# Spectral filter, small layers and first weight unit placed earlier among the conditioning units of a macaron DiT layer's first stage

## The reference

```python
mx = [m[:, None, :] for m in jnp.split(jax.nn.silu(c) @ ada_w[l] + ada_b[l], N_MOD, axis=-1)]
mc = jnp.split(jax.nn.silu(c_ctx) @ ada_w[l] + ada_b[l], N_MOD, axis=-1)
...
x = x + 0.5 * mx[2] * _swiglu(_modulate(_rmsnorm(x, norm_ffn1[l]), mx[0], mx[1]),
                              ffn1_w1[l], ffn1_w3[l], ffn1_w2[l])
...
# _hyena_spectrum
hid = jnp.sin(freq * (z @ w1 + b1))
hid = jnp.sin(freq * (hid @ w2 + b2))
hid = jnp.sin(freq * (hid @ w3 + b3))
h = (hid @ w_out).reshape(n, 2, 2, HY_WIDTH)
...
l1 = jnp.sum(jnp.abs(h_fwd), axis=0) + jnp.sum(jnp.abs(h_bwd), axis=0)
filt = jnp.concatenate([h_fwd, jnp.zeros((1, 2, HY_WIDTH), F32), h_bwd[::-1]], axis=0) / l1
return jnp.fft.rfft(filt, axis=0)
```

## Time and profile before

| what | value |
|---|---|
| runs of the kernel before | 3018.55, 3019.62, 3019.79 us (median 3019.62) |
| the profiled execution, as timed | 3019.63 us |
| span of its profile | 3017.8 us |
| TensorE matmuls busy | 2969.1 us, 98% of the span |
| VectorE, ScalarE, GpSimd busy | 68%, 38%, 5% |
| DMA over the span | 559.07 MB, mean 185 GB/s |
| granted TensorE clock, mean | 0.997 |

### The profile page before, as it was taken

One profiled execution on the slowest core, in us unless ns is written; L12 is line 12 of the kernel. 1 busy time (PEld: TensorE's weight loads), 2 busy tenths in 40 slices (PEclk: granted clock), 3 DMA queues, 4 the chain that ended last, 5 costly groups with the idle time before them and its releaser, 6 DMA issues. The chain is left out here.

```text
span 3017.8 us, 42600 instructions
## 1 busy us (share of the span) xinstructions
PE 2969.1 (98%) x15878; PEld 2528.7 (84%) x15878; DVE 2049.1 (68%) x2663; ACT 1160.7 (38%) x1477; POOL 147.7 (5%) x181
## 2 busy tenths in 40 slices
PE   7999999999999999999999999999999999999998
PEld 3588888888888888888889999999998888888886
DVE  4598667676766677673477767778866666666667
ACT  4332222222222222222248777754345444444444
POOL 1000000000000000000000033430000000000001
PEclk9999999999999999999999999999999999999999
DMA  9965546354466758563345554555565666666664
GB/s 370 327 209 188 181 134 202 128 178 146 157 221 221 255 168 282 186 228 102 95 98 167 171 166 148 153 152 180 158 203 168 188 192 190 188 193 189 189 193 147
DMA packets 369856, 559.07 MB, mean 185 GB/s; under 512 B 18175, under 2 KB 260216, under 8 KB 368840
## 3 DMA queue, kind: packets, MB, share of 16 engines
q1 hardware_dynamic: 364112, 544.62, 56.6%
q0 software_dynamic: 2640, 8.52, 0.9%
q10 hardware_dynamic: 2984, 4.29, 0.4%
HBM read 551.06 MB, written 6.30 MB: 185 GB/s over the span
## 5 line engine op out<-in xcount | busy, mean ns | idle before, releaser
L438 DVE TENSOR_TENSOR w_lo<-raw,w_hi 128x1024 fp32r<-128x1024 f32 x736 | 912.6, 1242 | 677.4 <-ACT w_hi L431 675.9
L431 ACT ACTIVATE w_hi<-raw 128x1024 fp32r<-128x1024 f32 x736 | 777.5, 1059 | 1484.2 <-PE bank L450 1093.6
L684 DVE SCALAR_TENSOR_TENSOR states<-ada_raw,silu_c,states 128x1024 f32<-128x1024 f32 x300 | 375.4, 1280 | 2.3
L448 PE MATMUL bank<-h_hi_early,w_hi 128*128 128x512 f32 x768 | 300.7, 391 | 1.0 <-issue 1.0
L450 PE MATMUL bank<-h_hi_early,w_lo 128*128 128x512 f32 x768 | 298.9, 389 | 0.0
L449 PE MATMUL bank<-h_lo_early,w_hi 128*128 128x512 f32 x768 | 298.8, 389 | 0.0
L448 PE MATMUL bank<-hx_hi,w_hi 128*128 128x256 f32 x1024 | 295.2, 288 | 0.0
L450 PE MATMUL bank<-hx_hi,w_lo 128*128 128x256 f32 x1024 | 289.6, 283 | 0.0
L449 PE MATMUL bank<-hx_lo,w_hi 128*128 128x256 f32 x1024 | 289.6, 283 | 0.0
L454 PE MATMUL bank<-w_hi,h 128*128 128x512 f32 x736 | 287.7, 391 | 1.9 <-DVE h L532 1.3
L456 PE MATMUL bank<-w_lo,h 128*128 128x512 f32 x736 | 286.5, 389 | 0.0
(11 more groups left out here) (341 smaller groups left out, 4815.0 us busy)
## 6 DMA issues: line engine op xcount, KB each, us to landing
raw<-in_ffn_w_dram SPq DMA_DIRECT2D x528, 512.0 KB, 4.1
ada_raw<-in_ada_w_dram SPq DMA_DIRECT2D x252, 512.0 KB, 4.5
raw<-in_w_in_dram SPq DMA_DIRECT2D x176, 512.0 KB, 3.8
raw<-in_w_out_dram SPq DMA_DIRECT2D x32, 512.0 KB, 3.6
ada_ahead<-in_ada_w_dram SPq DMA_DIRECT2D x20, 512.0 KB, 16.3
raw<-in_ada_w_dram SPq DMA_DIRECT2D x8, 512.0 KB, 18.7
ada_more<-in_ada_w_dram SPq DMA_DIRECT2D x8, 512.0 KB, 8.0
spec<-spec_spill POOLq DMA_DIRECT2D x8, 512.0 KB, 4.0
```

Of the source, the lines that this page charges most:

```text
L431: nc.scalar.activation(w_hi[un.slot(j)][:], raw[un.slot(j)][:], ACT.Copy).then_inc(hi_done, 1)
L438: nc.vector.tensor_tensor(w_lo[un.slot(j)][:], raw[un.slot(j)][:], w_hi[un.slot(j)][:].bitcast(F32), ALU.subtract).then_inc(lo_done, 1)
L448: nc.tensor.matmul(o, w_hi[slot][:, c0:c0 + P], hi, start=start, stop=False, skip_group_check=True)
L684: nc.vector.scalar_tensor_tensor(out=total, in0=src, scalar=silu_c[:, m, t:t + 1], in1=total, op0=ALU.mult, op1=ALU.add).then_inc(done, 1)
```

## The change

- SyncE's queue: the inputs of the small layers (`emb`, `fw1`, three loads into `fw23`) leave ScalarE's queue and stand ahead of `xin`. `window` and `dft` move from behind eight conditioning units to behind two; `yin` moves from behind four to behind ten. The first six weight loads stand behind units 36, 40, 45, 51, 56 and 61.
- The loop starts at step -4, so that the first two small layers and all groups of `x` come ahead of, or around, unit 0; the groups of `ctx` move to steps 12 and 13.
- `SPEC_AT` goes from (10, 18, 28, 36) to (4, 14, 22, 30), and all steps of a quarter follow at fixed distances from it. The fourth `l1_norm` and `inverse` move from inside the first weight unit to steps 38 and 39.
- `TAIL` goes from 48 to 44: the first weight unit comes four conditioning units sooner. The 20 units left over go in pairs behind k-groups 0, 1 and 2 of weight units 0 and 1, and 0 and 2 of weight units 2 and 3. `MOD_FIRST` goes from 37 to 35, and the first rounding steps move by two.
- `tokens` of `ctx` now waits for the first quarter's banks, squares of `ctx` use one buffer instead of two, and the first transpose waits for `emb` and `fw1` too (they share its semaphore).

```diff
-SPEC_AT = (10, 18, 28, 36)
+SPEC_AT = (4, 14, 22, 30)
...
-        FIRST_LOADS_AT = (39, 41, 45, 50, 56, 62)
+        FIRST_LOADS_AT = (36, 40, 45, 51, 56, 61)
...
             sy.dma_start(ident[:], i["t_ident"]).then_inc(c_in, 16)
+            sy.dma_start(emb[:], i["t_emb"]).then_inc(c_in, 16)
+            sy.dma_start(fw1[:], i["filt_w1"][0]).then_inc(c_in, 16)
+            sy.dma_start(fw23[:, 0, :], i["filt_w2"][0]).then_inc(mlp_in, 16)
+            for r in range(2):
+                sy.dma_start(fw23[:, 1 + r, :], i["filt_w3"][0]).then_inc(mlp_in, 16)
             sy.dma_start(xin[:], i["x"][0].rearrange("(a p) d -> p a d", p=P)).then_inc(x_in, 16)
-            for g in range(4):
-                load_wide(sy, g)
-            sy.dma_start(yin[:], i["ctx"][0].rearrange("(a p) d -> p a d", p=P)).then_inc(y_in, 16)
-            for g in range(4, 8):
+            for g in range(2):
                 load_wide(sy, g)
             sy.dma_start(window[:].rearrange("p a c -> p (a c)"), i["t_window"]).then_inc(window_in, 16)
             sy.dma_start(dft[:], i["t_dft"]).then_inc(window_in, 16)
-            for g in range(8, 10):
+            for g in range(2, 10):
                 load_wide(sy, g)
+            sy.dma_start(yin[:], i["ctx"][0].rearrange("(a p) d -> p a d", p=P)).then_inc(y_in, 16)
...
-        LAYER_AT, ANGLES_AT, SINE_AT = (2, 4, 8), (2, 4, 8), (4, 7, 11)
-        TOKENS_AT, EVICT_AT = (4, 4, 6, 6, 8, 8, 10, 10), (4, 4, 6, 6, 8, 8, 10, 10)
+        LAYER_AT, ANGLES_AT, SINE_AT = (-4, -2, 1), (-4, -2, 1), (-3, -1, 2)
+        TOKENS_AT, EVICT_AT = (0, 0, 1, 1, 12, 12, 13, 13), (0, 0, 1, 1, 12, 12, 13, 13)
...
-        TAIL = 48
-        L1_AT, INVERSE_AT = (20, 28, 37), (21, 29, 38)
...
-        MOD_FIRST = 37
-        FIRST_ROUND_AT = (41, 43, 45)
+        TAIL = 44
+        L1_AT, INVERSE_AT = (12, 22, 30, 38), (13, 23, 31, 39)
+        MOD_FIRST = 35
+        FIRST_ROUND_AT = (39, 41, 43)
+        INSIDE = {(0, 0): 44, (0, 1): 46, (0, 2): 48, (1, 0): 50, (1, 1): 52, (1, 2): 54, (2, 0): 56, (2, 2): 58, (3, 0): 60, (3, 2): 62}
...
             def turn(n, after):
-                pe.wait_ge(after, 48 if n == 3 else SMALL)
+                pe.wait_ge(after, 80 if n == 3 else SMALL)
...
+                if g == 8:
+                    pe.wait_ge(fs_out, 4)
...
-            for o in range(TAIL):
+            for o in range(LAYER_AT[0], TAIL):
...
-            ac.dma_start(emb[:], i["t_emb"]).then_inc(mlp_in, 16)
-            ac.dma_start(fw1[:], i["filt_w1"][0]).then_inc(mlp_in, 16)
...
-            ac.dma_start(fw23[:, 0, :], i["filt_w2"][0]).then_inc(mlp_in, 16)
-            for r in range(2):
-                ac.dma_start(fw23[:, 1 + r, :], i["filt_w3"][0]).then_inc(mlp_in, 16)
```

More of the change, by code:

```diff
@@ L1325, in layer @@
                     pe.wait_ge(fm_sin, n)
[L1326 to L1327 removed]
+                if n < 2:
+                    pe.wait_ge((c_in, mlp_in)[n], (80, MLP_SMALL)[n])
                 weights = fw1[:] if n == 0 else fw23[:, 0, :] if n == 1 else fw23[:, 1:3, :].rearrange("p a c -> p (a c)")
@@ L1362, in to_columns @@
                     pe.wait_ge(c_split, 2)
-                    pe.wait_ge(fm_sin, 3)
-                elif nth < 3:
-                    pe.wait_ge(fs_inv, (4, 8)[nth - 1])
+                if nth < 3:
+                    pe.wait_ge(fs_inv, (2, 6, 8)[nth])
                 for b in range(4):
@@ L1373, in raw_taps @@
                     pe.wait_ge(fm_sin, 3)
+                    pe.wait_ge(tr_out, 8)
+                else:
                     pe.wait_ge(tr_out, 16)
-                else:
                     pe.wait_ge(fs_out, 4 * q - 2 + 2 * a)
@@ L1385, in l1_norm @@
                 pe.wait_ge(fs_asum, 2 * q + 2)
-                if q == 1:
+                if q == 2:
                     pe.wait_ge(n1["rstd"], 2)
-                elif q == 3:
-                    pe.wait_ge(fs_inv, 6)
-                else:
-                    pe.wait_ge(ada_out, (2, 0, 3)[q])
+                elif q:
+                    pe.wait_ge(ada_out, (0, 2, 0, 3)[q])
                 for blk in range(4):
@@ L1430, in _ @@
                     l1_norm(L1_AT.index(o))
-                unit(o)
+                if o >= 0:
+                    unit(o)
             def inside(j, k):
-                g = TAIL + 4 * j + k
-                if k in (0, 2) and g < ADA_UNITS:
-                    unit(g)
-                    unit(g + 1)
-                if (j, k) == (0, 3):
-                    l1_norm(3)
+                if (j, k) in INSIDE:
+                    unit(INSIDE[j, k])
+                    unit(INSIDE[j, k] + 1)
                 if (j, k) == (1, 1):
@@ L1715, in square_tokens @@
                 if n >= 2:
-                    ac.wait_ge(n1["sq"], n - 1)
-                nc.scalar.activation((sq2 if n % 2 else xn2)[:], src, ACT.Square, accum_out=tok_sq[:, n:n + 1]).then_inc(n1["sq"], 1)
+                    ac.wait_ge(n1["sq"], n if n >= 4 else n - 1)
+                nc.scalar.activation((sq2 if n in (1, 3) else xn2)[:], src, ACT.Square, accum_out=tok_sq[:, n:n + 1]
+                                     ).then_inc(n1["sq"], 1)
             def row_out(nth):
@@ L2196, in _ @@
                 for n in range(2):
-                    if (q := step_of(WINDOW_AT, o, n)) is not None:
+                    if (q := spec_step(o, 1 + 2 * n)) is not None:
                         window_taps(q, n)
                 for n in range(2):
-                    if (q := step_of(SPECTRUM_AT, o, n)) is not None:
+                    if (q := spec_step(o, 5 + 2 * n)) is not None:
                         spectrum(q, n)
-                if o in TABS_AT:
-                    tabs_sum(TABS_AT.index(o))
+                if (q := spec_step(o, 6)) is not None:
+                    tabs_sum(q)
                 if o in INVERSE_AT:
```

23 lines of the change are left out of this document (6 added, 17 removed).

## The result

| | before | changed |
|---|---|---|
| median, us | 3019.7 (3017.82 to 3020.23, 8 runs) | 3028.36 (3026.88 to 3030.11, 8 runs) |
| ratio | | 1.0031, 95% interval 1.0022 to 1.0040 |
| span of the profiled execution, us | 3017.8 | 3026.8 |
| end of units 54 and 55 ("the point"), us | 120.65 | 130.18 |
| span less the point, us | 2897.2 | 2896.6 |

What follows compares the result with a forecast made beforehand. TensorE and the stream of loads both run at their limit, and the stream sets the stage's end. Less the later start, the point moves from 120.65 to 117.7, 2.95 rounded to 3.0 us: 3019.62 becomes 3016.6 us, range 3014.0 to 3020.0.

Steps and rivals of the forecast that it cites:

- The count at the point: Behind units 54 and 55 the work is the same, so the kernel's end moves by as much as this point.
- The start of the stream: Five small loads ahead of `xin` delay the large loads by 1.7 us, five times 0.43 less a quarter given back.
- Rival A: Start and clock eat the gain: `xin` 3.3 us later, one half-rate stretch costing 1.7 us; 3019.9 us, chance 0.13.
- I take it that TensorE has 4 to 8 us less idle time: Up to unit 43: at its own pace TensorE would finish it at 89 to 93 us instead of 95.76.
- For unit 10, behind `yin`: Early conditioning units: TensorE's wait for this load, named as an example of new short waits, without its own size.
- With the stream full, no order of loads makes it land sooner: Unit 55 lands at 114.9 us at the earliest, so the point comes at 116.0 at the earliest, gaining 4.7 us.
- Is ready near 93: First weight unit: VectorE's modulation starts near 78 us, takes 14.4 us, and is hidden by the wait for unit 43.
- The rule weighed: Skill's rule that waits between short bursts halve TensorE's clock, at 85 to 99 us; judged not to apply.
- the row at 108 us: Kernel before: TensorE works in short pieces between transfer waits, yet its clock is 1.00, the 2.4 GHz level.
- Rival B: The stream of loads can run faster, at 410 GB/s, winning 3.2 us more, 6.2 us in all; 3013.4 us, chance 0.07.
- Rival D: VectorE's modulation comes no sooner, so the first weight unit starts at about 101.97 as before; 3018.4 us, chance 0.06.
- Rival C: Layer 1 waits for bias columns on ScalarE's queue, tokens 16.8 us later, kernel 6.8 us slower; 3026.4 us, chance 0.06.

Runs made afterwards that it cites:

- Run 1: The kernel before with only the five small-layer loads moved to SyncE's queue ahead of `xin`: 3020.98 us, ratio 1.0004.
- Run 5: The changed kernel with the context's roots, exps and diagonal rows two steps later and `bounds_rest` with its lanes three steps later: 3021.79 us, ratio 1.0011.
- run 11: Run 9 with the context's load behind units 10 and 11 instead of ahead of them: 3021.51 us, ratio 1.0008.
- run 9: Run 5 with `x` loaded ahead of the five small loads instead of behind them: 3021.95 us, ratio 1.0010.
- Run 7: The changed kernel with the stage's last part and quarters 1 to 3 as before, roots, exps and diagonal rows two steps later: 3024.53 us, ratio 1.0016.
- run 10: Run 5 with the first weight unit back at conditioning unit 48, as before: 3022.62 us, ratio 1.0013.
- run 12: Run 5 with `x` first, the context's load behind unit 11 and the first weight unit at 48: 3022.13 us, ratio 1.0011.
- run 8: The kernel before with only the first weight unit, its loads and rounds two conditioning units sooner (46, not 48): 3018.02 us, ratio 0.9999.
- run 14: Run 5 with the five small loads on ScalarE's queue ahead of the biases: 3026.78 us, ratio 1.0027.

## Why the prediction was wrong

- **The count at the point: right.** The end moves by as much as units 54 and 55 move: 9.5 us at the point, 9.0 in the span.
- **"The start of the stream ... I take 1.7": right in size.** Run 1 shows 1.95 at the point and 1.82 at the first taps. The five issues took 3.43 us (2.35 to 5.78), 0.53 to 0.75 each, not SyncE's 0.43, so `xin` was issued 3.65 us later. Of that about half was given back, not a quarter of a smaller cost; that the two errors cancel is luck. Rival A had this at 3.3.
- **"I take it that TensorE has 4 to 8 us less idle time": the step that failed.** It was counted to unit 43 as if nothing but loads could hold TensorE. Up to the point it has 5.5 us more idle time, and its work takes 4.0 us more at half rate. The new waits are for ScalarE and VectorE, 2.34, 1.59, 1.73 and 4.1 us. The prediction went through TensorE's and SyncE's orders, and not through what stands ahead of `row_out` on ScalarE or ahead of an inverse on VectorE. Run 5 shows that the first two of these and what follows from them are 5.5 of the 8.7 us (6.0 by the ratios).
- **"For unit 10, behind `yin`" as a "new short wait": wrong in size, 7.29 us.** It could have been worked out: tokens, tables, context and 12 units are 12 MB, which takes 30 us at 396 GB/s, and 34 at the 348 GB/s that the kernel before moved up to 40.19 us, plus a start. But run 11, made on run 9, takes the wait away and gains nothing.
- **"With the stream full, no order of loads makes it land sooner": the condition failed.** The stream is full only as long as buffers come free. Unit 26 was used 14 us later than before, and the stream ran dry. Run 5 splits this: 7.3 us go with the two edits (unit 36 issued at 75.41 instead of 82.69), and the 6.8 us that stay, with the quarters ahead and the wait for unit 10, leave no gap there. With one delay alone unit 36 is issued at 81.37 or 81.41 and the gap stays, which fits that the points gain more from both edits (7.2) than from each alone (1.2 and 2.1). That the gap is how short waits turn into lasting loss is argued from this, and not shown. Run 7 comes nearest to parting the two: with a wait of 3.4 us and half clock behind it, but a nearly full stream (share 0.83 from 76 to 84 us), its point is still 3.6 us later than run 5's; its quarters and its first weight unit stand elsewhere, though.
- **"Is ready near 93": 109.99.** The length was nearly right (13.0 us from first modulation to first finished weight unit, against the forecast's 14.4). The start was not: `to_columns` came at 92.10 instead of 78, as TensorE was late. A first weight unit that VectorE releases was one of the prediction's own signs of being wrong; that is what happened. Only with the clock and the gap cured (run 5) does this become the limit, and putting units in its place (run 10) doesn't help.
- **The rule weighed.** The prediction let the row at 108 us speak against rival A's half rate. The rows show: behind waits of 7.29, 2.34 and 4.1 us the granted clock is on its 1.2 GHz level, behind 1.05 and 0.91 us (run 12, 96 to 100 us) it is not, and behind 1.59 us it isn't either. Between these it goes either way: 1.73 us at 100.62 were enough, 1.73 us at 93.82 in run 5 were not, and 1.99 us at the first taps were enough in the kernel before and not in run 8. So the Trainium skill (TensorE: Matmul & The Clock Gate, HAM oscillation) was right for the changed kernel: each of the long waits from 36 us on sent the clock back, and with some 23 us at half rate TensorE's work took 4.0 us longer. The row at 108 us had no wait over 1.00 us in it and said nothing on long ones. Rival A had one such stretch, at 1.7 us; there were four.
- **Rival B** (a faster stream) found nothing: the changed kernel moves 359 GB/s from 20 to 115 us, not 410. **Rival D** had VectorE releasing the first weight unit, at about 101.97 as before; VectorE did, but 8 us later, for a reason that D didn't have.
- **Rival C** (bias columns) didn't come about in the change, as the layers ran at 5.87 and 10.73 us. Its mechanism and its size did in run 14, where the order of the two was turned: 17.3 us of waiting.

What stays open: run 5 still costs 3.2 us, clear of none (1.0002 to 1.0020), and its point is 2.4 us later than before. Run 1 has 2.0 us for the small loads' start, which fits, but neither of two tries to take it back on the changed side did (run 9 puts the small loads behind `x`, run 14 the biases), so it is not shown there. In times alone run 1's cost can't be told from none. The places of the quarters (P) and the wait for unit 10 may have a part in it; no run has either alone.

## What to carry to other kernels

When work is moved ahead on one engine, walk the queues of all the engines that feed it, at each place where it now comes sooner: what stands ahead of the result there, and would be harmless at the old place (here a root, an exp, and two table loads; then 2.7 us of small column work). The longest wait in the list need not be where to begin. Here two runs took away 7.3 us of waiting for a transfer and won nothing, while the work behind waits of 2.3 and 1.6 us was worth 5.5: with it went the half clock behind them and a gap in SyncE's stream, for which buffers had come free too late.

And a bound of the kind "the loads set the end" holds only while every buffer is used in time. Check the last use that each load waits for along with the bytes.
